# Samples' attention with two value-product banks by turns, probabilities in the keys' ring of banks, and output additions behind the keys in two steps

## The reference, cut to what matters

```python
# per sample: q_lat (8 heads, 256), q_pe (8 heads, 64); cache read by pages
s = q_lat @ ckv.T + q_pe @ kpe.T            # past positions, and the new one
p = softmax(s * SM_SCALE)
o = p[..., :n_past] @ ckv_past + p[..., n_past:] @ ckv_new
```

## Time and profile before

| | |
|---|---|
| median of 3 runs | 2568.7 us (2567.85 to 2569.09) |
| profiled execution | 2569.62 us, span 2567.8 us |
| granted TensorE clock, mean over the span | 0.974 |
| PE busy | 2403.4 us (94%) |
| PEld busy | 2190.3 us (85%) |
| DVE busy | 1271.8 us (50%) |
| ACT busy | 767.7 us (30%) |
| POOL busy | 347.1 us (14%) |
| samples' attention | from 1356.93 us to about 1651 us of the span |

### The profile page before, as it was taken

How to read it: one execution, slowest core, us unless ns; L and a number is a source line. 1 busy time by engine, 2 the same in 40 slices (tenths; PEclk the granted TensorE clock), 3 DMA queues, 4 the chain that set the end, 5 groups by cost and what they waited for, 6 DMA issues and landing times.

```text
span 2567.8 us, 35295 instructions
## 1 busy us (share of the span) xinstructions
PE 2403.4 (94%) x14022; PEld 2190.3 (85%) x14022; DVE 1271.8 (50%) x2427; ACT 767.7 (30%) x1469; POOL 347.1 (14%) x308
## 2 busy tenths in 40 slices
PE   7899999999999968999998888898999999999997
PEld 7799999999999768899987667586998989999995
DVE  4624433333334665677768778534234433333335
ACT  2331111111111323555546556412311111111112
POOL 2400000000000420000006545023000000000006
PEclk9899999999999989999999999799999999999998
DMA  4021101111111031000005444411111111111111
GB/s 160 25 66 50 50 28 37 49 49 49 49 50 62 13 113 43 18 19 1 11 21 165 154 154 154 158 41 31 60 42 50 50 36 32 50 49 49 50 42 66
DMA packets 137073, 153.84 MB, mean 60 GB/s; under 512 B 10256, under 2 KB 114224, under 8 KB 136808
## 3 DMA queue, kind: packets, MB, share of 16 engines
q1 hardware_dynamic: 124656, 110.07, 13.6%
q0 software_dynamic: 12288, 41.95, 5.1%
HBM read 142.24 MB, written 10.32 MB: 59 GB/s over the span
## 4 chain that ended last, share of the span: by engine, by line
PE 82%; DVE 9%; ACT 4%; issue 3%; DMA 1%; POOL 1%; SPq 0%; POOLq 0%; ACTq 0%; DVEq 0%
PE ps L215 23%; PE ps L217 23%; PE ps L216 23%; DVE split L208 4%; ACT split L203 2%; PE ps L2079 2%; PE ps L2044 2%; PE ps L2059 1%; PE ps L223 1%; PE ps L222 1%; PE ps L2060 1%; PE ps L1589 1%; PE ps L2066 1%; PE ps L530 1%; DVE plain L1832 1%
## 5 line engine op out<-in xcount | busy, mean ns | idle before, releaser
L215 PE MATMUL ps<-split 128*128 128x512 f32 (+6 forms) x3632 | 1240.2, 341 | 64.8 <-DVE split L208 28.4
L217 PE MATMUL ps<-split 128*128 128x512 f32 (+6 forms) x3632 | 1225.7, 337 | 0.3 <-issue 0.3
L216 PE MATMUL ps<-split 128*128 128x512 f32 (+6 forms) x3632 | 1226.0, 338 | 0.0
L215 PEld LDWEIGHTS ps<-split 128*128 128x128 f32 x3632 | 692.9, 191 | 112.1 <-DVE split L208 34.6
L217 PEld LDWEIGHTS ps<-split 128*128 128x128 f32 x3632 | 693.0, 191 | 37.3
L216 PEld LDWEIGHTS ps<-split 128*128 128x128 f32 x3632 | 693.1, 191 | 36.5
L203 ACT ACTIVATE split<-plain 128x1024 fp32r<-128x1024 f32 (+7 forms) x446 | 313.5, 738 | 587.6 <-PE ps L223 362.1
L208 DVE TENSOR_TENSOR split<-plain,split 128x1024 fp32r<-128x1024 f32 (+7 forms) x422 | 359.2, 875 | 195.7 <-ACT split L203 192.6
L945 DVE TENSOR_TENSOR plain<-plain,ps 128x350 f32<-128x350 f32 (+1 forms) x132 | 68.1, 516 | 568.0 <-ACT plain L902 567.5
L275 DVE TENSOR_TENSOR plain<-plain,ps 128x512 f32<-128x512 f32 x360 | 245.0, 685 | 196.2 <-PE ps L217 191.4
L208 DVE TENSOR_TENSOR split<-ps,split 128x512 fp32r<-128x512 f32 (+5 forms) x480 | 247.3, 555 | 152.5 <-ACT split L203 145.1
(11 more groups left out here) (145 smaller groups left out, 1427.6 us busy)
## 6 DMA issues: line engine op xcount, KB each, us to landing
plain<-w_gate SPq DMA_DIRECT2D x44, 512.0 KB, 4.6
plain<-w_up SPq DMA_DIRECT2D x44, 512.0 KB, 4.1
plain<-w_down SPq DMA_DIRECT2D x44, 512.0 KB, 4.3
plain<-x_prompt SPq DMA_DIRECT2D x8, 512.0 KB, 11.2
x_spill<-plain SPq DMA_DIRECT2D x1, 4096.0 KB, 15.2
plain<-wo SPq DMA_DIRECT2D x8, 512.0 KB, 4.9
plain<-x_spill SPq DMA_DIRECT2D x8, 512.0 KB, 8.2
y_prompt<-plain SPq DMA_DIRECT2D x8, 512.0 KB
```

The costliest lines, as they stand in the source:

```text
L215: pe.matmul(out, still[0], moving[0], start=start, stop=False)
L216: pe.matmul(out, still[0], moving[1], start=False, stop=False)
L217: return pe.matmul(out, still[1], moving[0], start=False, stop=stop)
```

## The change

Three things are altered, all within the samples' attention.

1. The value products of a sample go to bank 4 or 6 by the sample's parity (`VALUE_BANKS`), so the first chunk of a sample waits for the additions of two samples before it (`do_steps` 4 (vb - 1)) and not of the sample before.
2. The bank for the turned probabilities (6) is given up; they take a place in the ring of four key banks, between the keys of step c = 2 and those of c = 3. `ring_tasks` lists the order, and `ring_free` waits for the user four places earlier. In ACT's and DVE's lists the split of the probabilities now stands behind all three key parts of step c = 2.
3. DVE's additions stand behind the three key parts; two of them at c = 3, two and the scaling at c = 4. `turn_output` and DVE's copy of it move from c = 4 to c = 5, `late` and what DVE takes of it from c = 4 to c = 6. The drain gets one more step.

No arithmetic instruction and no DMA is added or removed.

```diff
-SCORE_BANK, VALUE_BANK, SMALL_BANK, PROB_BANK, TAIL_BANK = 3, 4, 5, 6, 7
+SCORE_BANK, SMALL_BANK, TAIL_BANK = 3, 5, 7
+VALUE_BANKS = (4, 6)
+def ring_tasks():
+    tasks = []
+    for b in range(9):
+        for c in range(CHUNKS):
+            tasks += [("key", b, c, m) for m in range(3) if b < 8]
+            if c == 2 and b:
+                tasks.append(("prob", b - 1))
+    return tasks
+def ring_bank(*task):
+    return KEY_BANKS[RING_AT[task] % 4]
+def ring_free(pe, k, *task):
+    n = RING_AT[task]
+    if n < 4:
+        return
+    old = RING[n - 4]
+    if old[0] == "key":
+        pe.wait_ge(k.s["kt_lo"], 3 * (CHUNKS * old[1] + old[2]) + old[3] + 1)
+    else:
+        pe.wait_ge(k.s["dpt_lo"], old[1] + 1)
...
-    for c in range(LAG + 2):
+    for c in range(LAG + 3):
         step(9, 1, c, False, False, c < LAG)
...
-            if vb:
-                pe.wait_ge(s["do_steps"], 4 * vb)
+            if vb >= 2:
+                pe.wait_ge(s["do_steps"], 4 * (vb - 1))
...
     def turn_probs(b):
         pe.wait_ge(s["dexp"], b + 1)
-        if b:
-            pe.wait_ge(s["dpt_lo"], b)
+        ring_free(pe, k, "prob", b)
...
-        if c == 4 and output_of(b):
+        if c == 5 and output_of(b):
             turn_output(b - 2)
-        if c == 4 and softmax_of(b):
+        if c == 6 and softmax_of(b):
             late(b - 1)
...
         if keys:
             key_hi(0)
+        if keys:
+            key_hi(1)
+            key_hi(2)
         if c == 2 and softmax_of(b):
...
-        if keys:
-            key_hi(1)
-            key_hi(2)
...
         if keys:
             key_lo(1)
             key_lo(2)
+        if c == 2 and softmax_of(b):
+            dve.wait_ge(s["dpt_hi"], b)
+            lo_part(dve, k.prob_t[:, :, 64:128], prob_rows(k, b - 1).rearrange("p (i n) -> p i n", i=4),
+                    k.prob_t[:, :, 0:64]).then_inc(s["dpt_lo"], 1)
+        if c in (LAG, LAG + 1) and output_of(b):
+            dve.wait_ge(s["dpv_done"], CHUNKS * (b - 1))
+            ps, rows, base = k.ps[:, VALUE_BANKS[b % 2], :], k.out_rows, 4 * (b - 2)
+            if c == LAG:
+                dve.wait_ge(s["late_taken"], 2 * (b - 1))
+                dve.tensor_tensor(rows, k.new_out, ps[0:8, 0:256], ALU.add).then_inc(s["do_steps"], 1)
+                dve.wait_ge(s["do_steps"], base + 1)
+                dve.tensor_tensor(rows, rows, ps[0:8, 256:512], ALU.add).then_inc(s["do_steps"], 1)
+            else:
+                for n, part in ((2, ps[64:72, 0:256]), (3, ps[64:72, 256:512])):
+                    dve.wait_ge(s["do_steps"], base + n)
+                    dve.tensor_tensor(rows, rows, part, ALU.add).then_inc(s["do_steps"], 1)
+                dve.wait_ge(s["do_steps"], base + 4)
+                dve.tensor_scalar(rows, rows, k.sum_inv, None, ALU.mult).then_inc(s["out_norm"], 1)
```

More of the change, by code:

```diff
@@ L1913, with prob_rows @@
 KEY_BANKS = (0, 1, 2, 7)
-SCORE_BANK, VALUE_BANK, SMALL_BANK, PROB_BANK, TAIL_BANK = 3, 4, 5, 6, 7
+SCORE_BANK, SMALL_BANK, TAIL_BANK = 3, 5, 7
[8 more added lines that the diff above has]
+    return tasks
+RING = ring_tasks()
+RING_AT = {task: n for n, task in enumerate(RING)}
+def ring_bank(*task):
[9 more added lines that the diff above has]
+        pe.wait_ge(k.s["dpt_lo"], old[1] + 1)
+def prob_rows(k, b):
+    return k.ps[:, ring_bank("prob", b), 0:256]
 def page_index_dve(dve, k):
@@ L2014, in decode_pool, with key_part @@
         load(u)
-def key_part(k, u_c, m):
+def key_part(k, b, c, m):
     w = 256 if m == 2 else 512
-    bank = KEY_BANKS[(3 * u_c + m) % 4]
+    bank = ring_bank("key", b, c, m)
     return k.ps[:, bank, 0:w], k.key_t[:, 0, m * 512:m * 512 + w], k.key_t[:, 1, m * 512:m * 512 + w]
@@ L2037, in turn_keys @@
         for m in range(3):
[L2038 to L2041, removed]
+            ring_free(pe, k, "key", b, c, m)
+            ps = key_part(k, b, c, m)[0]
             for i in range(2 if m == 2 else 4):
@@ L2056, in scores @@
             pe.wait_ge(s["kt_lo"], 3 * u + m + 1)
-            _, hi, lo = key_part(k, c, m)
+            _, hi, lo = key_part(k, b, c, m)
             if m < 2:
@@ L2074, in values @@
             pe.wait_ge(s["dpt_lo"], vb + 1)
-            if vb:
-                pe.wait_ge(s["do_steps"], 4 * vb)
+            if vb >= 2:
+                pe.wait_ge(s["do_steps"], 4 * (vb - 1))
         pe.wait_ge(s["dc_lo"], v + 1)
         for i in range(4):
-            mm = pe.matmul(k.ps[0:72, VALUE_BANK, :], k.prob_t[:, i, 8 * vc:8 * vc + 72], k.values[:, slot, vc, i, :],
+            mm = pe.matmul(k.ps[0:72, VALUE_BANKS[vb % 2], :], k.prob_t[:, i, 8 * vc:8 * vc + 72], k.values[:, slot, vc, i, :],
                            start=vc == 0 and i == 0, stop=vc == CHUNKS - 1 and i == 3)
@@ L2100, in turn_probs @@
         pe.wait_ge(s["dexp"], b + 1)
-        if b:
-            pe.wait_ge(s["dpt_lo"], b)
+        ring_free(pe, k, "prob", b)
         wait_apart(pe, k)
         for i in range(4):
-            mm = pe.transpose(k.ps[:, PROB_BANK, i * 64:(i + 1) * 64], k.probs_s[:, i * P:(i + 1) * P], k.ident[0:64, 0:64])
+            mm = pe.transpose(prob_rows(k, b)[:, i * 64:(i + 1) * 64], k.probs_s[:, i * P:(i + 1) * P], k.ident[0:64, 0:64])
         mm.then_inc(s["dp_turned"], 1)
@@ L2178, in key_hi @@
                 act.wait_ge(s["kt_used"], 3 * (u - 1) + m + 1)
-            src, hi, _ = key_part(k, c, m)
+            src, hi, _ = key_part(k, b, c, m)
             hi_part(act, hi, src).then_inc(s["kt_hi"], 1)
@@ L2187, in step @@
                 act.wait_ge(s["dpv_done"], CHUNKS * (b - 1))
-            hi_part(act, k.prob_t[:, :, 0:64], k.ps[:, PROB_BANK, 0:256].rearrange("p (i n) -> p i n", i=4))\
+            hi_part(act, k.prob_t[:, :, 0:64], prob_rows(k, b - 1).rearrange("p (i n) -> p i n", i=4))\
                 .then_inc(s["dpt_hi"], 1)
-        if keys:
-            key_hi(1)
-            key_hi(2)
         if c == 0 and keys:
@@ L2232, in key_lo @@
             dve.wait_ge(s["kt_hi"], 3 * (CHUNKS * b + c) + m + 1)
-            src, hi, lo = key_part(k, c, m)
+            src, hi, lo = key_part(k, b, c, m)
             lo_part(dve, lo, src, hi).then_inc(s["kt_lo"], 1)
[L2236 to L2253, removed]
         if keys:
@@ L2265, in step @@
                .then_inc(s["max_tiled"], 1)
[L2266 to L2269, removed]
         if keys:
```

## The result

| | before | changed |
|---|---|---|
| median, four runs each | 2568.89 us | 2548.10 us (2545.22 to 2553.22) |
| ratio | | 0.9922, 95% interval 0.991 to 0.9934 |
| profiled execution, span | 2569.62, 2567.8 | 2545.22, 2543.4 |

The changed kernel is 0.8% faster; 2548.2 was the sum of the prediction, 2548.0 its number. In two later comparisons its ratio was 0.9914 (0.9897 to 0.993) and 0.9921 (0.9907 to 0.9935). Its runs lie 8 us apart, so that the traced one, the fastest of the first four, gained 24.4 us in its span while the median gained 20.8.

The account below looks back on a forecast made before the run. TensorE was taken to set the pace, with 3.75 us idle per 34.43 us sample. Gains 18.6 + 0.7 + 1.2 = 20.5 us from 2569.6 gave 2549.1, less 0.9 for the median 2548.2; predicted 2548, 8-in-10 range 2543 to 2555.

Parts of the forecast that it names:

- The unnamed 1.68 us: Idle time before the values of step 3, with no named releaser; the second value bank was to save 1.85 us there.
- Probabilities behind the keys: Step 3, before the scores: with the probabilities' split behind all key parts, a wait of 1.10 us per sample goes.
- `turn_output` and `late` apart: Step 4: the 0.56 us in which `late` waits for DVE's copy of the turned output goes.
- What DVE gives back: Steps 3 to 6: additions delay DVE's cache and key splits, so PE waits and loses 0.45 us per sample.
- Rival B: DVE becomes the bound in steps 3 to 6, costing 1.5 to 2.5 us per sample: 2552 to 2560, chance 0.17.
- its two signs: In steps 4 to 6 DVE idles less than 0.2 us, and PE waits over 1 us on it.
- Six samples: Samples b = 2 to 7: each loses 2.99 + 0.56 - 0.45 = 3.1 us, 18.6 together.
- Sample 1: The first wait in small form, 0.27 us before the last transposes and a like one before it: 0.7 us saved.
- The drain: After the last samples: sample 7's values start 1.75 us earlier, and 1.2 us is gained, bounds 0 to 3.
- C: Values of step 3: the second bank brings nothing because another wait ends at the same place; 2560.5 us, chance 0.03.
- D: The gathers on POOL become the bound, three waits of 0.6 us per sample: 11 us, 2559, chance 0.05.
- E: Projection behind the drain: PE's clock stays at 1.2 GHz, making the kernel slower by over 0.2%; chance 0.02.

Follow-up runs that it names:

- one-bank run: Changed kernel with both VALUE_BANKS entries 4, values waiting for the previous sample's additions, all additions at c = 3: 2586.81 us, 36.2 to 37.5 us a sample.
- banks-alone run: Kernel before the change with only the two value banks and the ring added, lists and steps as before: 2567.82 us, 34.36 us a sample.
- late-with-output: Changed kernel with `late` back behind the turned output, both at c = 5: 2565.78 us, 34.08 us a sample.

## Why the prediction was right, point by point

*What bounds it.* Right: in the samples TensorE was the bound with 3.75 us of waits. The three waits went, a sample took 31.20 us (31.3 forecast), and neither the gathers (no L2080 row released by a DMA from sample 1 on) nor DVE became the bound.

*Waits and who ends them.* The unnamed 1.68 us was read as the additions because their end lay 0.1 us before the values' start. The one-bank run shows the wait again, and the banks-alone run shows it gone. The prediction booked the whole 1.85 us to the second bank. That is right only in the company of the other two edits: with the ring and nothing else it gave 0.07. The prediction did not ask this of the part alone.

*Probabilities behind the keys.* 1.10 us forecast; step 3 in the whole gained 2.84 where 2.99 was said, since its keys still take 1.38 us. Here the prediction misread the ring: the turned probabilities now stand between the keys of steps 2 and 3, so the second key part of step 3 needs the middle low part of step 2, and the third part the last and not the middle one. The middle one ends at 1455.74 and the second key part starts at 1455.80, later than it would by the pace of the transposes before it. So "the ring's new neighbour costs nothing" is wrong by about 0.1 us, and a late split of the probabilities costs more with the ring than without (1.27 us against 0.88).

*`turn_output` and `late` apart.* 0.56 us was booked. Steps 4 to 7 took 15.39 us and take 14.99, 0.40 less: 0.56, less 0.06 because two steps' keys now follow small products where one did, less what DVE gives back. Against putting both at c = 5 the separation is worth 1.3 where the clock holds and 2.9 where it falls, which the prediction did not reckon with.

*What DVE gives back.* 0.45 us by the walk through DVE's list. The key rows show 0.29 over a plain step (0.13 in step 3, 0.16 in step 6), of which the walk explains about 0.1: step 3's is the ring's, and 0.06 of step 6's are the small products before it. Where it would show, in step 6, was right; its size was a quarter. Rival B falls with this, but it was near: of its two signs the first came, as DVE idles 0.14 us in steps 4 to 6, and the second, over 1 us of waits on it, did not; the additions in one step already cost 1.1 us per sample. Its lower end, 2552, does not follow from its price either: 1.5 in place of 0.45 for six samples makes 2554.5.

*Six samples.* 18.6 forecast, 19.4 measured; what DVE gives back was the term that was too large.

*Sample 1.* 0.7 forecast, nothing measured: from the first keys to the first values 38.3 us in both. This term failed. No values stand before the keys of that step, so TensorE comes to them 0.93 us earlier than in other samples; and in the ring their first part waits for the first part of the keys before, one place later than it did. The trace shows one idle time in front of the whole step where the kernel before had small ones inside it:

```profile
1393.36 1.38 PE L2080 MATMUL ps<-plain 128*128 128x128 f32 x10 [0.77 <-DVE split L208]
```

*The drain.* 1.2 us forecast, 4.2 measured in the first trace. The order was right (TensorE 1.7 us earlier, then DVE as the last to finish: additions at 1620.27, values done at 1617.98), the size was not, because the walk took every product at 1.2 GHz. With the clock fallen, as in a later trace of the same kernel, the drain takes 20.1 us and the gain is 2.0. In that trace `late` ends 2.2 us later after the last turned probabilities, and DVE's five head splits and the additions follow `late`. So some 2 us of the drain's gain hang on a clock that is not the same in every run.

*The sum.* That the median, 2548.10, meets the sum, 2548.2, to 0.1 us is luck in part: the runs lie 8 us apart, and terms missed by 0.7 to 3.0 us and made up for each other. What is borne out is the mechanism in the samples, which is nine tenths of the forecast gain and repeats in every trace of the changed kernel to 0.05 us.

*Rivals.* C is refuted by the one-bank run. The Trainium skill (TensorE: Matmul & The Clock Gate, HAM oscillation — how this bites in real kernels) tells of a kernel in which PSUM double-buffering gave nothing further. The banks and the ring alone agree with that (0.07 us), the whole change does not (3.23). D did not come, though its mechanism stirs: in a sample's stretch the rotary key's issue on POOL takes longer, and its idle time falls, but no gather is waited for. GpSimd's groups over the sample of the earlier trace rows before are 0.945 us for that issue, and after:

```profile
L2034 POOL DMA_INDIRECT plain<-cache_kpe,block_now x8 | 10.5, 1310 | 2.4 <-issue 2.4
```

It goes with the pace and not with the order of VectorE's list: its mean is 0.95 us in the banks-alone, the late-with-output and the one-bank run (34 to 37.5 us a sample), 1.12 with all additions at once and 1.29 with the probabilities between the keys (32.3 and 32.5), and 1.25 in the kernel before itself where gathers set the pace (1362 to 1384 us). The Trainium skill (GPSIMD Engine Reference, Specifications) says that GpSimd shares its SBUF interfaces with VectorE and contends with instructions of two SBUF inputs. At a faster pace both VectorE's share of the time and the closeness of the issues rise, so no run here tells which of them lengthens the issue. E, the clock, had a real mechanism in the wrong place: from the tail's products to the end the changed kernel's traces take 920.2 to 923.5 us and the one of the kernel before 921.7, but in the middle of the samples two experiments ran into a fallen clock.

## What to carry to other kernels

A second buffer removes a wait only if nothing else in the releasing engine's list stands in the same place: look up what the consumer's next instruction waits for, and by how much it is late, before counting the gain. When an engine that is busy 85% of the time must do extra work once per period, spread it over steps and put it behind what the bound engine needs next; here the order of the splits was worth 1.3 us of 34 and the spreading of the additions 1.1, each measured by taking it alone out of the changed kernel, and without the new lists the bank's gain did not come through. Time the parts of a kernel by landmarks inside its trace: 0.1 us in a period could be read where whole runs differed by 8.

## What the runs showed of the hardware

TensorE's clock fell from 2.4 to 1.2 GHz in the middle of the samples after 3.43 us idle (one bank; granted clock 0.62 over the next step). It also fell after 1.49 us idle with small products on both sides of it (late with the output; 1.00 until those behind it were done, 0.66 over the next step). Each fall cost 1.6 to 2.8 us on top of the wait. It did not fall after the 1.68 us of the kernel before, with the clock at 1.00 over the sample; nor, in the late-with-output run, in the sample b = 2, where the same instructions waited 1.48 us and the clock was 1.00 over the step behind. In the drain the clock was at 0.50 behind a wait of 0.99 us and behind one of 3.83, and the products took much the same time (4.42 and 4.62 us for twelve); there the same instructions ran at either level from run to run (1.14 or 1.98 us for four products). So a wait's price in such a loop can be about twice its length, and its length alone did not tell here when.
